# Z stage of a two-block decoder kernel: GpSimd makes all 28 weight subtractions, each in four pieces of 128x512

## The reference, cut to what matters

```python
h = rms_norm(x, g_mix)
z = einsum("bsd,de->bse", h, w_in) + b_in          # w_in: 1024 x 7168
va, ga, xb, gb, sa, sb = split(z, [1024, 1024, 1536, 1536, 1024, 1024])
u = causal_depthwise_conv(va * sigmoid(ga), conv_a_w, conv_a_b)      # 31 taps
v = causal_depthwise_conv(xb, conv_b_w, conv_b_b)                    # 4 taps
v = rg_lru(v, ...)   # a = exp(-8 r softplus(-lam)), scan h = a h + sqrt(1 - a^2) i v
y_b = einsum("bsc,cd->bsd", v * gelu(gb), w_b_out)
```

## Time and profile before

| | us |
|---|---|
| median of 3 runs | 1159.42 |
| lowest, highest run | 1159.11, 1169.11 |
| the profiled execution, its own time | 1171.32 |
| its span, first to last instruction | 1169.5 |

### The profile page before, as it was taken

The page is one execution under the profiler, slowest core; times in us unless marked ns, Lnnn a source line. Parts: engine busy times, 40 slices in busy tenths (PEclk is TensorE's granted clock), DMA queues, the critical chain, the costliest instruction groups (busy, mean ns, idle before and its releaser), DMA issues.

```text
span 1169.5 us, 18121 instructions
## 1 busy us (share of the span) xinstructions
PE 919.2 (79%) x7868; PEld 745.3 (64%) x7868; DVE 497.5 (43%) x784; ACT 369.0 (32%) x508; POOL 203.5 (17%) x76
## 2 busy tenths in 40 slices
PE   4988486856666665657588489998999989999996
PEld 4977476524233333333254389778999988888985
DVE  5434623411212120202021649999973446453541
ACT  4452411110101010101011434456656443534330
POOL 1031400000000000000000688702139820000000
PEclk9997585977889787978797889999999998999998
DMA  9850370999999999999998445424556643354510
GB/s 356 256 220 1 128 304 1 392 421 421 424 422 424 421 421 421 422 421 421 422 421 370 146 149 179 144 73 144 167 173 235 217 148 140 145 215 163 197 72 36
DMA packets 94891, 299.79 MB, mean 256 GB/s; under 512 B 9165, under 2 KB 45565, under 8 KB 86653
## 3 DMA queue, kind: packets, MB, share of 16 engines
q1 hardware_dynamic: 94125, 297.95, 65.7%
q0 software_dynamic: 576, 1.18, 0.4%
q10 hardware_dynamic: 144, 0.00, 0.0%
HBM read 298.07 MB, written 1.05 MB: 256 GB/s over the span
## 4 chain that ended last, share of the span: by engine, by line
PE 53%; DMA 25%; DVE 14%; ACT 4%; issue 2%; SPq 1%; POOL 0%; DVEq 0%; ACTq 0%; POOLq 0%
DMA mem<-in_w_up 22%; PE PS L1595 12%; PE PS L1596 11%; PE PS L1597 11%; PE PS L1749 9%; DVE PS L1425 6%; PE PS L1762 3%; DMA mem<-in_w 2%; PE PS L1588 1%; PE PS L1737 1%; ACT mlp_hi L963 1%; DVE ring_rest L1403 1%; ACT mem L660 1%; DVE HN L1125 1%; DVE mem L1382 1%
## 5 line engine op out<-in xcount | busy, mean ns | idle before, releaser
L1749 PE MATMUL PS<-mem 128*32 128x256 f32 x2048 | 156.1, 472 | 111.4 <-DMA mem<-in_w_up 110.1
L1597 PE MATMUL PS<-HT_hi,ring_rest 128*128 128x256 f32 x768 | 218.8, 285 | 0.0
L600 POOL TENSOR_TENSOR ring_rest<-mem,z_hi 128x2048 fp32r<-128x2048 f32 x21 | 98.4, 4691 | 619.1 <-ACT z_hi L803 540.6
L1749 PEld LDWEIGHTS PS<-mem 128*32 128x32 f32 x2048 | 83.8, 135 | 185.0 <-issue 163.5
L1597 PEld LDWEIGHTS PS<-HT_hi,ring_rest 128*128 128x128 f32 x768 | 148.6, 193 | 0.0
L1595 PE MATMUL PS<-HT_hi,z_hi 128*128 128x256 f32 x448 | 129.2, 288 | 9.9 <-ACT mem L865 5.7
L1596 PE MATMUL PS<-HT_rest,z_hi 128*128 128x256 f32 x448 | 128.4, 287 | 0.0
L1234 DVE TENSOR_TENSOR mem<-mem,PS 128x128 f32<-128x128 f32 x32 | 9.2, 287 | 241.9 <-ACT mem L776 241.9
L1539 DVE TENSOR_TENSOR ring_rest<-mem,mlp_hi 128x4096 fp32r<-128x4096 f32 x16 | 70.6, 4425 | 82.4 <-ACT mlp_hi L963 82.4
L1595 PEld LDWEIGHTS PS<-HT_hi,z_hi 128*128 128x128 f32 x448 | 87.7, 196 | 11.9 <-ACT mem L865 6.1
L1425 DVE SCALAR_TENSOR_TENSOR PS<-mem,CAW,PS 128x256 f32<-128x256 f32 x232 | 91.2, 479 | 0.0
(11 more groups left out here) (322 smaller groups left out, 1887.7 us busy)
## 6 DMA issues: line engine op xcount, KB each, us to landing
mem<-in_w_gate SPq DMA_DIRECT2D x32, 2048.0 KB, 15.2
mem<-in_w_up SPq DMA_DIRECT2D x32, 2048.0 KB, 19.7
mem<-in_w_down SPq DMA_DIRECT2D x32, 2048.0 KB, 12.0
mem<-in_w SPq DMA_DIRECT2D x16, 2048.0 KB, 7.9
mem<-in_w_in SPq DMA_DIRECT2D x28, 1024.0 KB, 5.3
mem<-in_w_in SPq DMA_DIRECT2D x5, 2048.0 KB, 19.3
mem<-in_w_b_out SPq DMA_DIRECT2D x4, 1536.0 KB, 8.7
mem<-in_w_out SPq DMA_DIRECT2D x2, 2048.0 KB, 15.0
```

The lines of the kernel that those rows point to most:

```text
L600: nc.gpsimd.tensor_tensor(z_rest(n), z_raw(n), z_hi(n).bitcast(F32), ALU.subtract).then_inc(z_rest_ready, 1)
L1597: ins = nc.tensor.matmul(dst, s_rest, m_hi, start=False, stop=stop and n == len(terms) - 1, skip_group_check=True)
L1749: ins = nc.tensor.matmul(PS[SLOTS * j:SLOTS * (j + 1), bank, 0:2 * F_STRIP].rearrange("p (w n) -> p w n", w=2), xg[:, k, :], w[:, :, k, F_ ...
```

## The change

`REST_LRU` and `REST_SCAN` go, and with them DVE's `rest_half` and its seven calls, POOL's waits for `lru_square`, `h_ready` and for DVE's `z_rest_ready`. POOL makes the rest of every half, in order, in four instructions of 128x512; only the last of the four raises `z_rest_ready`. That holds for halves 0 and 1 ahead of the stage as well. Loads, hi copies, matmuls and the late weights' subtractions (L636) stay as they are.

```diff
-REST_LRU, REST_SCAN = (16, 17, 18), (22, 23, 24, 25)
...
             def rest_half(n):
                 pool.wait_ge(z_hi_ready, n + 1)
-                nc.gpsimd.tensor_tensor(z_rest(n), z_raw(n), z_hi(n).bitcast(F32), ALU.subtract).then_inc(z_rest_ready, 1)
+                for part in range(4):
+                    at = slice(part * BLOCK, (part + 1) * BLOCK)
+                    ins = nc.gpsimd.tensor_tensor(z_rest(n)[:, at], z_raw(n)[:, at], z_hi(n)[:, at].bitcast(F32), ALU.subtract)
+                ins.then_inc(z_rest_ready, 1)
...
             for n in range(2, IN2_HALVES):
-                if n == REST_LRU[0]:
-                    pool.wait_ge(lru_square, RG)
-                if n == REST_SCAN[0]:
-                    pool.wait_ge(h_ready, RG)
-                if n not in REST_LRU + REST_SCAN:
-                    if n - 1 in REST_LRU + REST_SCAN:
-                        pool.wait_ge(z_rest_ready, n)
-                    rest_half(n)
+                rest_half(n)
...
-            def rest_half(n):
-                dve.wait_ge(z_rest_ready, n)
-                dve.wait_ge(z_hi_ready, n + 1)
-                nc.vector.tensor_tensor(z_rest(n), z_raw(n), z_hi(n).bitcast(F32), ALU.subtract).then_inc(z_rest_ready, 1)
...
-            rest_half(REST_LRU[0])
...
-                if g == 2:
-                    rest_half(REST_LRU[1])
...
-            rest_half(REST_LRU[2])
...
-                rest_half(REST_SCAN[g])
```

## The result

| | before | changed |
|---|---|---|
| median of the runs, us | 1162.49 (4 runs) | 1182.59 (4 runs) |
| ratio, 95% interval | | 1.0134, 1.0088 to 1.018 |
| the profiled execution, own time and span | 1171.32, 1169.5 | 1183.08, 1181.3 |

The account below looks back on a forecast made before the run. PE was taken to bound the z stage, its waits paid in full. Half 26 late 10.8, low clock 1.4, earlier start -1.6: +10.6 us on the median 1159.4 gives 1170.0 us; 8-in-10 range 1156 to 1176.

Parts of the forecast that it names:

- Sum: Whole kernel: 10.8 + 1.4 - 1.6 = +10.6 us, set on the median 1159.4, giving 1170.0 us.
- A + B: First product of the final norm to the next projection, through the z stage: +10.6 us forecast.
- Part 1: Ahead of the z stage: VectorE's two products end 4.2 us earlier, the stage begins 1.6 us earlier.
- A: Stretch from VectorE's first product of the final norm to the first z matmul; forecast 1.6 us shorter.
- Part 2: LRU phase: VectorE waits for about nine whole pieces, 22.0 us in all, ending 4.5 us later; PE doesn't see it.
- Part 3: Scan phase: VectorE's 20 operations wait for about 17 pieces of 1.17 us; last `h_ready` 17.7 us later, at 871.9.
- Part 4: Late `h_ready` holds `split_h` and ACT's take behind it: PE idle 12 us, half 26 10.8 us late, plus 1.4 for clock.
- Scans passing the port: Rival, scan phase: scans don't wait, or the port isn't handed over for each piece; -3.0 us, 1156.4; chance 0.20.
- VectorE keeping it: Rival, scan phase: VectorE keeps the port, GpSimd starves, halves 23 and 24 come late; +5 to +6, 1165 us; chance 0.13.
- pieces with a full start each: Rival: each piece costs a whole start, 1.41 us; last `h_ready` at 880, +20.7, 1180 us; chance 0.12.
- B: Stretch from the first z matmul to the next projection; forecast 12.2 us longer.

Follow-up runs that it names:

- second trace: The changed kernel profiled once more without an edit; timed 1.0119 (1.0076 to 1.0162) against the kernel before.
- eight pieces: The changed kernel with eight subtractions of 128x256 for each half in place of four of 128x512; timed 1.0094 (1.0054 to 1.0135) against the kernel before.

## Why the prediction was wrong

- **The base, 10 us of the 12.6.** The step that failed is in the paragraph "Sum": "the median lies 11.9 lower, in parts that the change doesn't touch, so I set it on the median". The change doesn't touch those parts, but they vary: the first product began between 645.5 and 658.9 us in 14 traces. The profiled execution at 1171.3 was of the group in which three quarters of the runs lie, and the median of three was of the other; with 35 runs it is 1169.67. The sum against the profiled execution, 1181.9, is 0.7 from what was measured, and that is luck in part: from profile to profile the changed kernel began its first product 4.1 us earlier, took 13.6 more in A + B, where 10.6 were forecast, and 2.3 more behind them. In the lower group the median of three would have been the right level: the changed kernel's one run apart took 1170.21. It has no trace, so whether it was of that group isn't shown.
- **Part 1, -1.6 forecast, +1.6 measured in A: 3.2 us.** The products (4.2 us earlier forecast, 4.0 measured) and the waits of the tiny products were right. What was left out is that GpSimd's memsets move with its pieces and that VectorE's row operations wait for them: 5.64 us in place of 2.58. The prediction had priced the later memsets by who uses their output, not by who shares the port. To this come 2.3 us of lower clock in most traces with such a start, for which the sum had no term.
- **Part 2, 22.0 us forecast, 809.02 - 787.36 = 21.7 measured, by another way.** Nine waits for a piece were counted. In the first trace the first four products had none, VectorE then stood 3.27 us for ACT's exponentials, and of the other eight one waited 0.3 us and seven about 1.0 each. So the 21.7 is near the forecast by luck. The second trace is nearer to the count: ten waits of 0.8 to 1.1 us, and 21.2 us in all.
- **Part 3, 35.3 us forecast, 868.0 - 834.4 = 33.6 measured.** Scans do take part: 1.70 us at the median in place of 0.67. That no row had shown it was the forecast's main doubt. A piece costs VectorE some 1.05 us (1.65 between scans less 0.6), though alone it takes 1.23; 1.17 was between them.
- **Part 4, right in place and order.** Half 26 was forecast 12 us late to start and 1.4 us slow; it waited 6.8 and 9.5 us, and two halves at the low clock cost 14.3 - 11.5 = 2.8. Half 26 came 9.3 us and 8.5 us later, counted from the first z matmul, than 862.5 - 676.8 = 185.7 of before; forecast were 10.8.
- **The rivals.** Scans passing the port, VectorE keeping it, and pieces with a full start each are all refuted by the changed kernel's own trace; the second came true with eight pieces, in part: there PE waited for GpSimd, 6.5 us in all, though VectorE didn't keep the port but took turns.

In sum B was forecast 12.2 us longer and was 11.0 and 11.9, of which 2.3 us of the 11.9 are the lower clock; A's sign was wrong; and the level on which the sum was set was a sample of three.

## What to carry to other kernels

When two engines share a port and take turns, one waits for at most one of the other's instructions with each of its own, and for no more of them than there are. So splitting one engine's instructions helps the other only once it makes more of them than the other has operations: four pieces left the scan phase at 33 us, eight made it 24 and made GpSimd late. Then follow who stands behind the last wait in an in-order queue. Moving an instruction moves everything behind it on that engine, memsets too, and each of them can meet someone new. Before a difference of one per cent is set on a median, see how far the executions of the unchanged kernel lie apart, and where; a stretch between two marks in the trace repeated here within 0.3 us in one kernel and 0.9 in the other, where the total moved by 10.

## What the runs showed of the hardware

- Alternation is not strict. In the LRU phase a piece that was taken up at 787.27 came to its end only at 792.07, 4.80 us for 1.27 of work, because four products of VectorE, back to back, went ahead of it. In the changed kernel's second trace the same four products took turns with the pieces, 1.76 to 2.05 us each, so the program alone doesn't decide it. Three scans back to back let a piece in between each. What makes the difference was not tried.
- The Trainium skill (SBUF — State Buffer, section "Who interferes with whom") has two-input VectorE instructions contend with GpSimd ones that read SBUF; the scan is one of them here (0.67 to 1.70 us), and so is a product of two elements a partition (0.16 to 1.19). A row operation with one tensor input met a memset, 2.8 us each for 1.25: the same section has VectorE's two-port modes contend with GpSimd, which this agrees with, though no row says in which mode the operation ran. Beside subtractions of 128x256 two took 3.38 us, where two alone take 2.50.
- A subtraction of 128x512 on GpSimd alone takes 1.27 us and follows the last one at 1.23; of 128x256, 0.70; of 128x2048, 4.53. In alternation a 128x512 costs VectorE only 1.05. That some of its start lies under VectorE's turn would explain this, and is not shown.
